# A new step order on TensorE, ScalarE and VectorE of a four-layer fp32 forward pass

## The reference

```python
def mla_mixer(h, ...):
    q_lat, kv_lat, k_rope, gate = split(h @ w_in)
    q = rmsnorm(q_lat, q_norm_g) @ w_uq          # 8 heads, 128 + 64 rotated
    kv = rmsnorm(kv_lat, kv_norm_g) @ w_ukv      # 8 heads, keys 128, values 128
    attn = block_causal_attention(q_nope, rot(q_rope), k_nope, rot(k_rope), v)
    return (attn * silu(gate)) @ w_out

def rglru_mixer(h, ...):
    u, gate = split(h @ w_in); uc = causal_conv(u, 4)
    r, i = sigmoid(uc @ w_rg + b_rg), sigmoid(uc @ w_ig + b_ig)
    a = exp(-8 * r * softplus(-lam)); b = sqrt(1 - a * a) * (i * uc)
    return (scan(a, b) * silu(gate)) @ w_out

def layer(x, mem):                                # twice
    z = rmsnorm(x) @ w_in
    o_mem = softmax(qm @ mk.T / 8) @ mv           # 4 heads of 64
    o_self = diff_or_causal_attention(z)          # layer 0: 6 heads, layer 1: 12
    x = x + concat(o_self, o_mem) @ w_out
    return x + relu(rmsnorm(x) @ w_up) ** 2 @ w_down
```

## Time and profile before

| | us |
|---|---|
| median of 3 runs | 816.03 (815.88 to 816.26) |
| span of the profiled execution, first to last instruction | 814.4 |
| PE busy | 801.8 (98%) |
| PE weight loads busy | 747.8 (92%) |
| VectorE busy | 602.5 (74%) |
| ScalarE busy | 550.7 (68%) |
| mean granted clock of TensorE | 0.998 |

### The profile page before, as it was taken

One profiled execution on the slowest core, in us unless ns is written; L12 is line 12 of the kernel. 1 busy time (PEld: TensorE's weight loads), 2 busy tenths in 40 slices (PEclk: granted clock), 3 DMA queues, 4 the chain that ended last, 5 costly groups with the idle time before them and its releaser, 6 DMA issues.

```text
span 814.4 us, 14821 instructions
## 1 busy us (share of the span) xinstructions
PE 801.8 (98%) x5854; PEld 747.8 (92%) x5854; DVE 602.5 (74%) x1140; ACT 550.7 (68%) x1045; POOL 0.2 (0%) x4
## 2 busy tenths in 40 slices
PE   8999999999999999999999999999999999999997
PEld 8989899999999899988989999998899888888886
DVE  7999997989987995876657475866757667564664
ACT  7876876699977888767455465668866756553652
POOL 0000000000000000000000000000000000000000
PEclk9999999999999999999999999999999999999999
DMA  9533344665564544464837365444434657554451
GB/s 329 191 103 130 105 147 144 201 201 169 182 202 130 175 137 130 155 226 137 281 117 248 130 238 178 130 133 153 149 111 157 211 177 236 188 175 167 166 181 52
DMA packets 40676, 137.83 MB, mean 169 GB/s; under 512 B 4640, under 2 KB 6176, under 8 KB 40608
## 3 DMA queue, kind: packets, MB, share of 16 engines
q1 hardware_dynamic: 39600, 135.70, 50.0%
q10 hardware_dynamic: 1008, 1.20, 0.4%
HBM read 135.83 MB, written 1.05 MB: 168 GB/s over the span
## 4 chain that ended last, share of the span: by engine, by line
PE 88%; DVE 9%; ACT 1%; issue 1%; DMA 1%; ACTq 0%; DVEq 0%
PE bank L796 15%; PE bank L803 15%; PE bank L798 14%; PE bank L797 14%; PE bank L804 7%; PE bank L807 5%; PE bank L809 5%; PE bank L808 5%; DVE weights_lo L1753 2%; PE bank L1171 2%; DVE temp L1753 1%; DMA weights_raw<-stream_dram 1%; DVE arena L1753 1%; DVE operand L1753 1%; DVE temp L1756 1%
## 5 line engine op out<-in xcount | busy, mean ns | idle before, releaser
L1753 DVE TENSOR_TENSOR weights_lo<-weights_raw,weights_hi 128x1024 fp32r<-128x1024 f32 (+3 forms) x257 | 299.7, 1191 | 37.1 <-ACT weights_hi L1249 36.7
L796 PE MATMUL bank<-operand,weights_hi 128*128 128x256 f32 (+1 forms) x1092 | 313.5, 287 | 1.6 <-DVE weights_lo L1753 1.0
L798 PE MATMUL bank<-operand,weights_lo 128*128 128x256 f32 (+1 forms) x1092 | 309.5, 283 | 0.0
L797 PE MATMUL bank<-operand,weights_hi 128*128 128x256 f32 (+1 forms) x1092 | 309.1, 283 | 0.0
L1249 ACT ACTIVATE weights_hi<-weights_raw 128x1024 fp32r<-128x1024 f32 (+3 forms) x257 | 257.3, 1031 | 76.2 <-PE bank L798 34.6
L796 PEld LDWEIGHTS bank<-operand,weights_hi 128*128 128x128 f32 x1092 | 206.1, 189 | 7.6 <-issue 5.0
L798 PEld LDWEIGHTS bank<-operand,weights_lo 128*128 128x128 f32 x1092 | 206.2, 189 | 0.0
L797 PEld LDWEIGHTS bank<-operand,weights_hi 128*128 128x128 f32 x1092 | 205.8, 188 | 0.0
L803 PE MATMUL bank<-operand,weights_hi 128*128 128x512 f32 x512 | 180.1, 394 | 0.0
L804 PE MATMUL bank<-operand,weights_lo 128*128 128x256 f32 x512 | 143.6, 281 | 0.0
L803 PEld LDWEIGHTS bank<-operand,weights_hi 128*128 128x128 f32 x512 | 96.2, 188 | 21.3
(11 more groups left out here) (212 smaller groups left out, 791.8 us busy)
## 6 DMA issues: line engine op xcount, KB each, us to landing
weights_raw<-stream_dram SPq DMA_DIRECT2D x242, 512.0 KB, 4.3
weights_raw<-stream_dram SPq DMA_DIRECT2D x6, 384.0 KB, 3.5
temp<-memT_dram SPq DMA_DIRECT2D x8, 256.0 KB, 5.2
weights_raw<-stream_dram SPq DMA_DIRECT2D x6, 256.0 KB, 5.7
residual<-xT_dram SPq DMA_DIRECT2D x6, 136.0 KB, 5.5
constants<-consts_dram SPq DMA_DIRECT2D x1, 536.5 KB, 6.9
arena<-consts_dram SPq DMA_DIRECT2D x1, 512.0 KB, 4.3
out_dram<-arena SPq DMA_DIRECT2D x2, 256.0 KB, 2.5
```

The source lines that it names most:

```text
L796: e.matmul(to, w_h, x_h, start=start, stop=False, skip_group_check=True)
L797: e.matmul(to, w_h, x_l, start=False, stop=False, skip_group_check=True)
L798: return e.matmul(to, w_l, x_h, start=False, stop=stop, skip_group_check=True)
L1753: return e.tensor_tensor(to, a, b, op)
```

## The change

No instruction is added or removed, and the order of the projections and of the transfers is the same. The numbers of TensorE's small steps no longer come from rules but from `TIMES`, as ScalarE's and VectorE's do, and nearly all numbers of the three engines are other ones. Code that this leaves unused is deleted.

```diff
-HEADS_STEPS = ((4.5, 6.5, 7.5), (5.5, 7.55, 8.5), (6.55, 8.55, 9.5), ...
-SLOTS_0 = ((7, 9, 11), (8, 10, 12), (13, 15, 18), ...
 TIMES = {
+    ("tensor", "mean"): (4.5, 7.333, 7.667, 30.5, 32.5, 69.5, 97.5, 161.5, 189.5),
+    ("tensor", "mla_scores"): (15.333, 15.667, 17.667, 18.75, 20.833, 20.333, 21.4, 21.6),
...
-    def tensor(time, *step):
+    def tensor(*step):
+        time = step[1] if step[0] == "project" else next(times["tensor", step[0]])
         table["tensor"].append((time, len(table["tensor"]), step))
...
-    def statistics(v, name):
+    def statistics(name):
         vector("total", name)
-        tensor(v + 0.95, "mean", name)
+        tensor("mean", name)
...
-        tensor(scored + 0.91, "scores", layer, kind, h)
+        tensor("scores", layer, kind, h)
...
-        tensor(turned + 0.93, "turn", layer, kind, h)
+        tensor("turn", layer, kind, h)
...
-        tensor(valued + 0.96, "values", layer, kind, h)
+        tensor("values", layer, kind, h)
```

More of the change, by code:

```diff
@@ new lines @@
+    ("tensor", "sub_turn"): (86.6, 90.5, 91.5),
+    ("tensor", "turn_residual"): (192.5, 194.5, 196.5, 198.5),
+    ("scalar", "root"): (8.5, 12.5, 12.75, 33.333, 36.5, 74.333, 101.5, 163.75, 193.333),
+    ("scalar", "row"): (9.5, 13.5, 14.5, 34.667, 37.25, 79.1, 74.667, 103.5, 165.5, 195.5),
+    ("scalar", "latent_hi"): (14.667, 14.167, 14.833, 15.8, 15.4),
+    ("scalar", "meta_latent"): (18.25, 16.5),
+    ("scalar", "small"): (6.5,),
+    ("scalar", "lambda_exp"): (14.333,),
+    ("scalar", "mla_softmax"): (19.833, 19.5, 20.571, 21.5, 24.5, 26.2, 26.3, 26.8),
@@ L356, in statistics @@
         vector("rstd", name)
-        tensor(v + 1.95, "spread", name)
+        tensor("spread", name)
         scalar("row", name)
@@ L360, in statistics @@
             scalar("row", "in2_0g")
-    held = {}
-    def hold(v, units):
-        for u in units:
-            held[u] = v
-    a = AT["a_in", 0, 0, 0]
-    statistics(a + 4, "a")
+    statistics("a")
     vector("rope_rows_a")
-    hold(a + 6.06, range(a + 3, a + 6))
-    statistics(a + 8, "q")
-    statistics(a + 8, "kv")
+    statistics("q")
+    statistics("kv")
     for m in range(5):
@@ L384, in timetable @@
         vector("small", i)
-    first = AT["a_uq", 0, 0, 0]
-    for h, (at, turned, valued) in enumerate(HEADS_STEPS):
-        at, turned, valued = first + at, first + turned, first + valued
-        tensor(at, "mla_scores", h)
+    for h in range(HEADS):
+        tensor("mla_scores", h)
         vector("mla_mask", h)
@@ L391, in timetable @@
         vector("mla_norm", h)
-        tensor(turned, "mla_turn", h)
+        tensor("mla_turn", h)
         scalar("mla_turned", h)
         vector("mla_turned", h)
-        tensor(valued, "mla_values", h)
+        tensor("mla_values", h)
         vector("mla_y", h)
@@ L411, in timetable @@
         vector("conv_rest", m)
-    for k0, m0 in ((0, 0), (0, 2), (4, 4), (4, 6)):
-        g = AT["gates", 0, k0, 1] + 1 + m0 % 4 // 2
+    for m0 in range(0, 8, 2):
         vector("inputs", m0)
@@ L431, in timetable, with head @@
         vector("y_b_rest", m)
-    def head(layer, kind, h, scored, turned, valued):
-        tensor(scored + 0.91, "scores", layer, kind, h)
+    def head(layer, kind, h):
+        tensor("scores", layer, kind, h)
         vector("softmax_first", layer, kind, h)
@@ L452, in diff_head @@
         vector("merge", h)
-        tensor(turned + 0.93, "turn", 0, "diff", h)
+        tensor("turn", 0, "diff", h)
         scalar("turned", 0, "diff", h)
-        tensor(valued + 0.96, "diff_values", h)
+        tensor("diff_values", h)
         scalar("diff_out", h)
     for layer in range(2):
-        i = AT["in2", layer, 0, 18]
-        statistics(i + 1, f"in2_{layer}")
+        statistics(f"in2_{layer}")
         vector("rope_rows_2", layer)
-        hold(i + 3.06, [i + 1])
         for h in range(MEM_HEADS):
-            head(layer, "mem", h, i + 3 + h // 2, i + 6 + h // 2, i + 8 + h // 2)
+            head(layer, "mem", h)
         if layer == 0:
             vector("scale_x")
-            for h, slots in enumerate(SLOTS_0):
-                diff_head(h, *(i + n for n in slots))
-            for group, t in enumerate((i + 14.3, i + 19.3, i + 22.1)):
+            for h in range(6):
+                diff_head(h)
+            for group in range(3):
                 vector("sub_mean", group)
@@ L473, in timetable @@
                 scalar("sub_scale", group)
-            for h, n in ((0, 18), (2, 22), (4, 23)):
-                tensor(i + n + 0.97, "sub_turn", h)
+            for h in range(0, 6, 2):
+                tensor("sub_turn", h)
                 scalar("sub_turn", h)
@@ L478, in timetable @@
         else:
-            for h, slots in enumerate(((8, 10, 12), (8, 10, 12), (9, 11, 13), (9, 11, 13),
-                                       (12, 14, 16), (12, 14, 16), (13, 15, 17), (13, 15, 17),
-                                       (18, 20, 21), (18, 20, 21), (19, 21, 22), (19, 21, 22))):
-                head(1, "moba", h, *(i + n for n in slots))
-        u = AT["up", layer, 0, 0]
-        statistics(u + 1, f"mlp_{layer}")
-        hold(u + 3.05, [u + 1])
+            for h in range(12):
+                head(1, "moba", h)
+        statistics(f"mlp_{layer}")
     for v in range(len(UNITS)):
-        w, time = UNITS[v], held.get(v, v + 1)
+        w = UNITS[v]
         parts = parts_of(w)
```

167 lines of the change are left out of this document (82 added, 85 removed), and 56 rows, old and new, of the table TIMES.

## The result

The changed kernel takes 810.33 us (median of four runs, 810.30 to 811.04) against 816.14 us before (four runs). The ratio is 0.9932, with a 95% interval from 0.9918 to 0.9946: 0.7% faster, a gain of 5.8 us. The span went from 814.4 to 808.5 us, so the whole 5.9 us are inside it.

A forecast was written before the change was run, and what follows sets the result against it. TensorE (PE) bounds the kernel, busy 801.8 of 814.4 us, with VectorE about level in the latent heads. Terms: 1.4 + 0.1 + 0.8 - 0.6 + 0 + 1.7 = 3.4 us off 816.03, so 812.6 us; range 810.9 to 816.0.

The forecast's parts named there:

- spread a: At the start, behind unit 5: TensorE's single wait on VectorE's rstd a goes whole, a gain of 1.4 us.
- unit 15 and latent heads: Holes at unit 15 and in the latent heads: gains of 0.1 us net and 0.8 us.
- recurrence: Between 113 and 250 us, where TensorE had no hole worth the name: a loss of 0.6 us.
- layer 0: Second block's layer 0, put together with both MLPs: 0, with 0.5 us to either side.
- layer 1: Memory heads' scores and values and one pair of causal values: holes go, a gain of 1.7 us.
- the wait for bank 7 at unit 54: In the recurrence, ScalarE empties bank 7 later: TensorE waits 0 to 1.1 us, taken as 0.6.
- the latent scores: In the latent heads: their wait on finish, given as 0.7 us (0.9 with the starts), goes.
- The three holes that I had named: In layer 1: memory heads' scores 0.7 us, their values 0.9, and 0.16 at 572.40, all to go.
- the sum of all holes that I knew, with none new: Rival over the whole kernel: all holes go and none comes, 5.1 us gained, 810.9 us; chance 0.10.
- VectorE eats the early gain: Rival: early gain lost where VectorE and ScalarE set the pace, about 814.9 us; chance 0.23.
- stalls in line: Rival: VectorE's strict list stalls in the latent heads, making the kernel slower, 818.0 us; chance 0.10.
- the condition of the prediction, 1.9 us up to 113 us: From 24 to 113 us, VectorE's idle time needs to fall from 4.2 to 1.9 us.

The follow-up runs named there:

- start alone: Kernel before with only the start's steps (series part 1, rstd a, root a, ScalarE's small step) in the new order: 815.42 us, ratio 0.9997.
- start and heads: Kernel before with all steps of old number below 33 (start through latent heads, first memory norm, mean b) in the new order: 813.10 us, ratio 0.9965.
- the run with pairs: Changed kernel with the turns of causal heads 1, 5 and 8 of layer 1 put next to their neighbour's turn: one execution, span 808.3 us.
- layer 0 alone: Kernel before with only the steps of old numbers 69 to 96 (norm, memory and differential heads of layer 0) in the new order: 815.57 us, ratio 0.9995.

## Why the prediction was wrong

In the order of its terms (leads between units, counted from unit 5):

| term | forecast | measured |
|---|---|---|
| `spread a` | 1.4 | 1.45 at unit 6 |
| unit 15 and latent heads, less losses up to unit 24 | 0.9 | 2.72 - 1.45 = 1.27 |
| units 24 to 33 | 0 | 0.47 |
| recurrence, units 33 to 70 | -0.6 | 0.0 |
| layer 0, units 70 to 97 | 0 | 3.71 - 3.19 = 0.52 |
| units 97 to 161 | 0 | 0 |
| layer 1 | 1.7 | 2.42 |
| MLP and end | 0 | 0 |

- *Right:* what bounds the kernel, the largest hole with its size and cause, its survival, that the latent heads keep what they gain, that layer 1 gains most, and that the MLPs and the end are neutral. `spread a` was argued to 0.05 us from rows, and the one run that left it out gave 1.41.
- *The recurrence, the largest error (0.6 us).* The step that failed is the wait for bank 7 at unit 54: the forecast let ScalarE come earlier either by TensorE's 2.3 us or by the 0.72 us of the step taken out, and took the middle. The two add up. `evacuate` 48 starts at 183.71 instead of 187.70, 4.0 us earlier, where TensorE is 3.0 us earlier (200.69 - 197.69). The runs show each part alone: with the step in its old place `evacuate` 48 comes 0.96 us earlier at 0.95 us of TensorE (start alone, 186.74) and 3.22 at 3.21 (start and heads, 184.48), so ScalarE follows TensorE in full; the moved step gives 1.0 us on top. The bank is free 1.2 us before TensorE wants it, and the wait is nothing.
- *Small holes that I had left out (1.0 us).* Units 24 to 33 had no term at all, and layer 0 was put at 0 although I knew of a few tenths there. Of the 0.47 us of units 24 to 33 about 0.25 lie at one start inside unit 24 (112.07 before) and about 0.2 around the `mean` of the memory norm; of the 0.52 us of layer 0, 0.36 lie between units 83 and 88, where TensorE had waited ahead of unit 86. The bound of 0.5 us to either side was meant for layer 0 and the MLPs, and did not cover the sum.
- *Unit 15, mis-sized by 0.5 us; the latent scores, by the wrong row.* Up to unit 17, where both kernels have done the same steps, the lead is 2.06 us, 0.6 more than at unit 6, where 0.1 was forecast; from there to unit 24 come 0.66 where 0.8 was. `finish` 14 moved by 1.3 us and not by 1.0 (55.15 instead of 56.48), and of the two holes of 1.1 us together one of 0.34 is left. Against that a hole of 0.3 us at unit 13 is new. In the latent heads the scores' hole went as said, but the 0.7 us of L1150 did not: 0.5 of them are still there. Timelines of PE and of DVE, kernel after (the x8 are `finish` 14 and, right behind it, `finish` 13):

```profile
55.69 0.47 PE L796 MATMUL bank<-weights_hi,operand 128*128 128x512 f32 x1 [0.17 <-issue]
```

```profile
55.15 2.87 DVE L1742 TENSOR_TENSOR operand<-bank,operand 128x272 fp32r<-128x272 f32 x8
```

- *Layer 1, mis-sized by 0.7 us.* The three holes that I had named measure 0.7, 0.9 and 0.25; by unit 173, where both kernels have done the same steps, the lead grew by 5.73 - 3.71 = 2.02. A further 0.4 us come behind it, for which I had looked up nothing: 0.3 between units 174 and 179 and 0.1 from there to unit 183. The pairs of turns, which I suspected, give 0.1 us at most by the run with pairs. In which of the small groups the rest lies is not settled.
- *The range.* Its lower end, 810.9, was the sum of all holes that I knew, with none new. It was too high because nothing stood in it for units 24 to 33 and 174 to 183 (0.47 and 0.4 us), and 0.3 for all of layer 0 and the MLPs, where 0.52 came. The rivals in which VectorE eats the early gain (0.23) and in which it stalls in line (0.10) rested on a busy share of 95%; the run of the start alone refutes the first. VectorE's idle time from 24 us to unit 24 did fall, from 85.57 - 81.35 = 4.2 to 83.04 - 79.93 = 3.1 us; the condition of the prediction, 1.9 us up to 113 us, was wrong, since busy time fell too. The two windows, of the kernel before and after:

```profile
24.00:109.57 85.57, 81.91 (x633) 77.34 (x632) 81.35 (x266) 63.84 (x162) 0.00 (x0) 1.00 0.35 118
```

```profile
24.00:107.04 83.04, 81.79 (x636) 77.44 (x634) 79.93 (x260) 65.94 (x165) 0.00 (x0) 1.00 0.39 122
```

On the rule of the Trainium skill, page "ScalarE: Activation LUTs", section "What ACT_TABLE_LOAD costs": it puts a drain of 1380 ns beside the load at every switch to another set. The trace after disagrees as the one before did: from the start of the load at 193.38 to the start of the activation at 194.67 there are 1.29 us, the load's own 1.28 and nothing else, and the activation ahead of the load ends at 193.36.

## What to carry to other kernels

In this kernel, whose engines do fixed lists and hand work to each other in a regular pattern, a hole that was taken out upstream shifted the whole pattern and stayed won to the end, even through a stretch in which the second engine was busy for 95% of the time: the busy share did not make it the bound. So sum all holes of the bounding engine, the small ones too. For a new wait, add up all that moves the engine that feeds it: its own lighter load and the lead that it takes over from the others. And of work that is not urgent ask which step stands right behind it in its line: one step of 0.48 us in the wrong place cost 0.77 us (half of it in a way that no wait explains), and 2.6 us elsewhere in the same stretch cost nothing. Closing a hole is no gain by itself: where the step that waited heads a chain, as `mla_values 1` does, moving it back lost 0.66 us.

## What I had not expected of the hardware

The start of unit 5 varied between 22.8 and 23.8 us over the traces, by the arrival of the first weights, and a start that was 0.57 us later was absorbed by the hole of `spread a` behind it (in the run of layer 0 alone, unit 6 began at 28.01 against 28.19). Differences of spans below 1 us between single executions therefore say little in this kernel; leads counted from unit 5 agree to 0.07 us between executions that share an order, except where such a hole takes up a late start, as in the run of layer 0. Nor had I expected a pause of 0.27 us inside one VectorE step that comes and goes with the place of four small instructions far ahead of it.
